# A two-block network on one core: VectorE scales the rows before the transposes, and a new order of the eight feature tiles

## What is computed

```
first network:   h = x
  layer 0        h += even_mixer(rms_norm(h));  h += swiglu(rms_norm(h))
  layer 1        h += odd_mixer(rms_norm(h));   h += moe_swiglu(rms_norm(h))     8 experts, top 2
                 x = rms_norm(h)
second network, twice:
                 x += 0.5 * rms_norm(swiglu(rms_norm(x)))        ("f1")
                 x += rms_norm(hybrid_mix(rms_norm(x)))          (the hybrid mixer)
                 x += 0.5 * rms_norm(swiglu(rms_norm(x)))        ("f2")

rms_norm(x, g) = x * rsqrt(mean(x*x) + 1e-6) * g       row by row
```

## Time and profile before

| | us |
|---|---|
| median of three runs | 2469.18 |
| the profiled execution | 2467.24 |
| its span in the trace | 2465.5 |
| PE busy | 2437.7 (99%) |
| DVE busy | 2034.6 (83%) |
| ACT busy | 1544.8 (63%) |

### The profile page before, as it was taken

The page is one execution under the profiler, slowest core; times in us unless marked ns, Lnnn a source line. Parts: engine busy times, 40 slices in busy tenths (PEclk is TensorE's granted clock), DMA queues, the critical chain, the costliest instruction groups (busy, mean ns, idle before and its releaser), DMA issues.

```text
span 2465.5 us, 39205 instructions
## 1 busy us (share of the span) xinstructions
PE 2437.7 (99%) x14162; PEld 2083.5 (85%) x14162; DVE 2034.6 (83%) x2978; ACT 1544.8 (63%) x2153; POOL 73.2 (3%) x158
## 2 busy tenths in 40 slices
PE   9999999999999999999999999999999999999998
PEld 8888887788888888888888888899888888898887
DVE  7777766889898989998999987789877877798776
ACT  6754555677777777777777764463644644644544
POOL 9000000000000000000000000000000000000000
PEclk9999999999999999999999999999999999999999
DMA  7466643699999999999999966643566566533663
GB/s 213 147 189 187 179 154 128 232 370 367 354 359 375 366 351 359 377 362 352 368 373 365 365 201 195 187 122 103 173 187 195 174 194 187 154 101 115 197 195 111
DMA packets 481949, 596.82 MB, mean 242 GB/s; under 512 B 21922, under 2 KB 313202, under 8 KB 481808
## 3 DMA queue, kind: packets, MB, share of 16 engines
q1 hardware_dynamic: 478208, 589.47, 71.4%
q0 software_dynamic: 3600, 5.48, 0.8%
HBM read 593.83 MB, written 1.05 MB: 241 GB/s over the span
## 4 chain that ended last, share of the span: by engine, by line
PE 91%; DVE 5%; ACT 2%; issue 1%; DMA 0%; SPq 0%; DVEq 0%; ACTq 0%
PE bank L893 25%; PE bank L654 16%; PE bank L919 12%; PE bank L688 10%; PE bank L660 8%; PE bank L639 5%; PE bank L636 2%; PE bank L1524 1%; DVE wlo_ring L2248 1%; PE bank L904 1%; PE bank L1241 1%; PE bank L1069 1%; PE bank L736 1%; PE bank L760 1%; DVE h L2598 1%
## 5 line engine op out<-in xcount | busy, mean ns | idle before, releaser
L2248 DVE TENSOR_TENSOR wlo_ring<-raw_ring,whi_ring 128x1024 fp32r<-128x1024 f32 (+1 forms) x1122 | 1331.3, 1219 | 116.0 <-ACT whi_ring L1616 96.0
L1616 ACT CAST whi_ring<-raw_ring 128x1024 fp32r<-128x1024 f32 (+1 forms) x1122 | 1145.5, 1051 | 165.2 <-DMA raw_ring<-in_od_exp_w_dram 153.3
L654 PE MATMUL bank<-x,whi_ring 128*128 128x512 f32 x1720 | 427.3, 391 | 0.0
L654 PEld LDWEIGHTS bank<-x,whi_ring 128*128 128x128 f32 x1720 | 315.6, 188 | 60.9
L660 PEld LDWEIGHTS bank<-x,wlo_ring 128*128 128x128 f32 x1720 | 220.9, 191 | 9.4 <-DVE wlo_ring L2248 1.0
L660 PE MATMUL bank<-x,wlo_ring 128*128 128x256 f32 x1720 | 223.8, 283 | 0.8 <-DVE wlo_ring L2248 0.8
L1690 ACT COPY arena<-bank 128x256 f32<-128x256 f32 x110 | 40.9, 372 | 268.8 <-PE bank L660 268.8
L639 PE MATMUL bank<-x,whi_ring 128*128 128x256 f32 (+2 forms) x1024 | 193.0, 289 | 0.7 <-DVE x L2326 0.6
L893 PE MATMUL bank<-whi_ring,xg0hi 128*128 128x512 f32 x448 | 178.3, 398 | 2.9 <-DVE xg0lo L2397 2.9
L893 PE MATMUL bank<-whi_ring,xg1hi 128*128 128x512 f32 x448 | 177.2, 395 | 0.0
L893 PE MATMUL bank<-whi_ring,xg0lo 128*128 128x512 f32 x448 | 175.5, 392 | 0.0
(11 more groups left out here) (540 smaller groups left out, 3576.0 us busy)
## 6 DMA issues: line engine op xcount, KB each, us to landing
raw_ring<-in_od_exp_w_dram SPq DMA_DIRECT2D x672, 512.0 KB, 5.5
raw_ring<-in_ffn_w_gate_dram SPq DMA_DIRECT2D x88, 512.0 KB, 3.9
raw_ring<-in_ffn_w_up_dram SPq DMA_DIRECT2D x88, 512.0 KB, 5.0
raw_ring<-in_ffn_w_down_dram SPq DMA_DIRECT2D x88, 512.0 KB, 3.5
raw_ring<-in_ev_ffn_w_dram SPq DMA_DIRECT2D x66, 512.0 KB, 4.0
raw_ring<-in_w_in_dram SPq DMA_DIRECT2D x42, 512.0 KB, 4.1
raw_ring<-in_od_w_in_dram SPq DMA_DIRECT2D x24, 512.0 KB, 4.3
raw_ring<-in_ev_w_in_dram SPq DMA_DIRECT2D x20, 512.0 KB, 7.0
```

The source lines that it names most:

```text
L654: mm_ = mm(bank[:, :], wh[:, kt, :], X2[:, kt, :, :].rearrange("p a n -> p (a n)"), start=(start and kt == 0), stop=(stop and kt == KT - 1 ...
L1616: nc.scalar.copy(WHI[:, slot, 0:n], RAW[:, slot, 0:n]).then_inc(s["hi_ready"], 1)
L2248: V_.tensor_tensor(WLO[:, slot, 0:n], RAW[:, slot, 0:n], WHI[:, slot, 0:n].bitcast(F32), ALU.subtract)\
```

## The change

- `norm` on DVE no longer writes `DIAG`. It writes the scaled rows themselves to `HN`, in two halves of 512 columns (128x512, two factors), each with an increment of the semaphore, which is renamed from `diag_ready` to `rooted`.
- PE turns `HN` by plain transposes (`turn_block`, 16 instructions), and waits for `rooted` before blocks 0 and 2 of each row tile.
- In the hybrid entries the squares of row tile 1 are made in two halves on ACT. DVE adds epsilon to the first half's sum (`y_mean`), ACT takes the root of the second half's sum with that as its bias. The first entry keeps whole tiles (`by_half=False`).
- `X_ORDER` becomes (0, 2, 1, 3, 4, 6, 5, 7), for every entry.

```diff
-X_ORDER = (0, 2, 4, 6, 1, 3, 5, 7)
+X_ORDER = (0, 2, 1, 3, 4, 6, 5, 7)
...
-            def turn_block(banks, t, b):
+            def turn_block(banks, t, b, rows=H):
                 for kt in (2 * b, 2 * b + 1):
                     last = tr(BANK[banks[b]][:, (2 * (kt % 2) + t) * P:(2 * (kt % 2) + t + 1) * P],
-                              H[:, t, kt * P:(kt + 1) * P], IDENT[:, :])
+                              rows[:, t, kt * P:(kt + 1) * P], IDENT[:, :])
...
                 for t in range(TT):
-                    pe.wait_ge(s["diag_ready"], nxt("diag_ready"))
-                    for last in turn_t(t):
+                    for b in range(4):
+                        if b % 2 == 0:
+                            pe.wait_ge(s["rooted"], nxt("rooted"))
+                        last = turn_block(TURNED, t, b, HN)
                         if t == TT - 1:
                             last.then_inc(s["tp_ready"], 1)
...
+            def norm_by_half(l):
+                act.wait_ge(s["h_ready"], nxt("h_ready"))
+                mean_square(0)
+                act.wait_ge(s["half_ready"], 5 + 3 * l)
+                af(HN[:, 1, 0:512], H[:, 1, 0:512], ACT.Square, scale=D ** -0.5, accum_out=STAT[:, 1:2])\
+                    .then_inc(s["y_ssq"], 1)
+                act.wait_ge(s["h_ready"], nxt("h_ready"))
+                af(HN[:, 1, 512:D], H[:, 1, 512:D], ACT.Square, scale=D ** -0.5, accum_out=STAT[:, 24:25])\
+                    .then_inc(s["ssq_ready"], 1)
+                act.wait_ge(s["y_mean"], nxt("y_mean"))
+                act.wait_ge(s["ssq_ready"], nxt("ssq_ready"))
+                af(STAT[:, 35:36], STAT[:, 24:25], ACT.Sqrt, bias=STAT[:, 25:26]).then_inc(s["root_of_ssq"], 1)
...
-            def norm():
+            def norm(by_half=True):
                 for t in range(TT):
-                    dve.wait_ge(s["ssq_ready"], nxt("ssq_ready"))
-                    link(V_.tensor_scalar(STAT[:, 36 + t:37 + t], STAT[:, t:t + 1], EPS, None, ALU.add))
+                    if t and by_half:
+                        dve.wait_ge(s["y_ssq"], nxt("y_ssq"))
+                        V_.tensor_scalar(STAT[:, 25:26], STAT[:, 1:2], EPS, None, ALU.add).then_inc(s["y_mean"], 1)
+                        dve.wait_ge(s["ssq_ready"], nxt("ssq_ready"))
+                        link(V_.tensor_scalar(STAT[:, 37:38], STAT[:, 24:25], STAT[:, 1:2], EPS, ALU.add, ALU.add))
+                    else:
+                        dve.wait_ge(s["ssq_ready"], nxt("ssq_ready"))
+                        link(V_.tensor_scalar(STAT[:, 36 + t:37 + t], STAT[:, t:t + 1], EPS, None, ALU.add))
                     dve.wait_ge(s["root_of_ssq"], nxt("root_of_ssq"))
                     y, c_ = inverse_root(STAT[:, 34 + t:35 + t], 36 + t, 0.5, 1.5)
-                    V_.tensor_scalar(DIAG[:, t, :], IDENT[:, :], y, c_, ALU.mult, ALU.mult).then_inc(s["diag_ready"], 1)
+                    for h in range(2):
+                        hs = slice(h * 512, (h + 1) * 512)
+                        V_.tensor_scalar(HN[:, t, hs], H[:, t, hs], y, c_, ALU.mult, ALU.mult).then_inc(s["rooted"], 1)
```

More of the change, by code:

```diff
@@ L183, in build @@
         names = """hi_ready lo_ready chunk_used bank_free silu_ready hidhi_made
-        hid_ready half_ready gate_lo gate_sum gate_ready up_lo rx_mm rx_made row_root gate_order lrt_ready hid_made h_ready y_ready y_half ssq_ready root_of_ssq y_ssq y_gained y_mean root_of_y diag_ready tp_ready xhi_ready x_ready ident_ready first_tp first_ready consts_ready cols_tp cols_ready
+        hid_ready half_ready gate_lo gate_sum gate_ready up_lo rx_mm rx_made row_root gate_order lrt_ready hid_made h_ready y_ready y_half ssq_ready root_of_ssq y_ssq y_gained y_mean root_of_y rooted tp_ready xhi_ready x_ready ident_ready first_tp first_ready consts_ready cols_tp cols_ready
         loads_done gbc_used dve_order pool_order router_ready msk_ready pos_mm flag_ready
@@ L692, in spread_roots @@
             def spread_roots():
-                pe.wait_ge(s["diag_ready"], nxt("diag_ready", 2))
+                pe.wait_ge(s["rooted"], nxt("rooted", 2))
                 for t in range(TT):
@@ L2223, in _ @@
                 post(f1)
-                norm()
+                norm_by_half(l)
                 gain(f"mix_pre{l}")
@@ L2300, in ffn_roots @@
                         link(V_.scalar_tensor_tensor(ROOT_D[t], y, c_, ROOT[t], ALU.mult, ALU.mult))
-                        V_.tensor_copy(ROOT[t], ROOT_D[t]).then_inc(s["diag_ready"], 1)
+                        V_.tensor_copy(ROOT[t], ROOT_D[t]).then_inc(s["rooted"], 1)
                         V_.tensor_scalar(ROOT_D[t], ROOT_D[t], D ** -0.5, None, ALU.mult)
                     else:
-                        V_.tensor_tensor(ROOT[t], y, c_, ALU.mult).then_inc(s["diag_ready"], 1)
+                        V_.tensor_tensor(ROOT[t], y, c_, ALU.mult).then_inc(s["rooted"], 1)
                         link(V_.tensor_scalar(ROOT_D[t], y, c_, D ** -0.5, ALU.mult, ALU.mult))
@@ L3261, in _ @@
                 dve.wait_ge(x_loaded[t], 16)
-            norm()
+            norm(by_half=False)
             dve.wait_ge(s["first_ready"], 1)
```

## The result

The changed kernel takes 2473.64 us (median of 20 runs) against 2468.43 us of the kernel before (20 runs): ratio 1.0022, 95% interval 1.0016 to 1.0028, which is 5.4 us more, 3.9 to 6.9 (the two medians differ by 5.2). The profiled execution has a span of 2473.1 us. All medians are of runs in the chip's fast state; one run of e9 (2675.51 us at a granted clock of 0.849) was in the slow one and isn't counted.

What follows compares the result with a forecast made beforehand. PE, busy 99% of the span, bounds the long products, but DVE's chain paces the entries. Plain entries 2.82, experts' leave -0.05, hybrid entries 1.22 and first entry 0.82 sum to +4.8 us: 2469.18 to 2474.0, range 2469.0 to 2478.0.

Steps and rivals of the forecast that it cites:

- What bounds the entries: Ahead of `gain` in a hybrid entry: PE late by only 0.46 us, then DVE's chain sets the pace.
- The write of 512 columns: DVE's write of half a row tile's scaled rows in `norm`: 541 ns, two halves holding DVE 0.91 us instead of 0.26.
- D: Rival: DVE's 512-column write runs at one element a cycle, +2.1 us, 2476.1; chance 0.11.
- The order: `gain` with the new tile order: DVE stands 0.23 us twice, +0.47 in each of six plain entries, 2.82 together.
- B: Rival: slack behind the entries makes the gaps of the new order vanish, +1.0 us, 2470.2; chance 0.15.
- The hybrid entry: Two hybrid entries: first copy of `gain` 0.31 us later through DVE's queue, 0.30 more from the order; +1.22 together.
- The first entry: First entry: longer writes and weight splits put the first subtraction at 11.57 against 11.12, plus two order gaps; +0.82 us.
- rival C: TensorE's clock falls to half in transpose-only stretches of rooted entries, one to three times at about 0.8 us: 2475.6; chance 0.22.
- a stretch of few products: On the path to the experts: said to precede the granted clock's fall to 0.50 at 437.30 to 440.70.
- The 0.2% taken as the border: Whole kernel: a measurement tells about 0.2%, 4.9 us, from no change, putting the border between same and slower at 2474.1.

Runs made afterwards that it cites:

- e9: Kernel before with row tile 0 half by diagonal, half by scaled rows, row tile 1 all by scaled rows, order (0, 2, 4, 1, 6, 3, 5, 7): 2467.64 against 2467.82 us.
- e7: Changed kernel with PE doing row tile 0's eight transposes twice in each of the three rooted entries: 2475.05 us, a single execution read for its trace.
- e10: Changed kernel as it is, profiled once more: 2474.39 us, a single execution read for its trace.
- e3: Kernel before with order (0, 1, 2, 3, 4, 5, 6, 7), each odd tile right behind its even neighbour: 2491.98 against 2468.09 us, ratio 1.0098.
- e4: Kernel before with order (0, 2, 4, 1, 6, 3, 5, 7), two other tiles between neighbours: 2467.27 against 2468.09 us, ratio 0.9998.
- e2: Kernel before with only the new order (0, 2, 1, 3, 4, 6, 5, 7): 2474.07 against 2468.09 us, ratio 1.0022.
- e1: Changed kernel with the old order (0, 2, 4, 6, 1, 3, 5, 7) put back: 2469.78 us against 2468.09 for the kernel before, ratio 1.0008.
- e5: Changed kernel with DVE making `y_mean` ahead of row tile 0's writes in the hybrid entries: 2472.86 us, a single execution read for its trace.
- e8: Changed kernel without PE's unread products (`keep_busy`) ahead of the hybrid entries: 2472.88 us, a single execution read for its trace.
- e6: Kernel before, old order, with only row tile 1 by scaled rows and plain transposes, row tile 0 by diagonal: 2467.31 against 2467.15 us, ratio 0.9998.
- e11: Kernel before as it is, profiled once more: 2468.08 us, a single execution read for its trace.

## Why the prediction was right

*What bounds the entries:* right. PE was late by about half a microsecond only, and the saved half of its turning time came back as idle time (0.68 before the first release then, 0.88 and 1.08 now). e7 shows it directly.

*The write of 512 columns:* 541 ns predicted; the median of the twelve is 544, and two in a row take 1.00 us, so they start 0.46 apart. D, with 0.75, falls.

*The order:* 0.47 a plain entry predicted; 0.45 to 0.50 measured in all but the second dense entry (and the router's wider stage in e10). e3 shows the same wait at full size, e4 that a place more removes it. B, the free order, falls by e2.

*The hybrid entry:* 0.61 predicted, 0.65 and 0.66 measured; the rows alone give 0.19 (e1) and the order alone 0.40 (e2), 0.59 together. The step by step working holds too: from DVE's first write to ACT's root 1.09 worked out and 1.10 measured, to the first copy 3.24 and 3.27. That ACT's half squares would wait for the bias behind DVE's writes is plain in the trace (1.14 idle) and e5 takes it away.

*The first entry:* 0.82 predicted, 0.79 and 0.86 measured. The working put the first subtraction 3.96 behind DVE's first write (11.57 less 7.61); e10, which starts at 7.61 as before did, has 3.99. In the first profile it starts at 11.55, but there DVE began at 7.50, so 4.05 behind: the near match of that clock time, and of 0.79, has luck in it.

*Where it was short:* the sum was 4.8 and the traces give 5.2 and 5.4, the timed runs 5.4 with their interval. That the forecast of 2474.0 lies only 0.4 from the measured 2473.64 is partly luck: it started from 2469.18, the median of three runs, where twenty give 2468.43, and this 0.75 made up for the 0.4 to 0.6 that the sum lacked. Two things are outside the sum. First, the second dense entry lost 0.72 instead of 0.47. The extra 0.25 is DVE standing 0.28 us ahead of its update of `H`, behind one of its own small instructions:

```profile
1761.05 1.41 DVE L2621 SCALAR_TENSOR_TENSOR h<-arena,stat,h 128x512 f32<-128x512 f32 x2 [0.28 <-DVE stat L2617]
```

It stands at the same place, 0.28 each time, in e1, e7, e8 and e10, and in none of before, e2 to e6, e9 and e11. e9 has a like stand of 0.34 at another place (ahead of L3019 at 1645.75, behind DVE's own copy). It comes again with the same kernel and no wait of the code explains it; its cause stays open. Second, the clock: rival C was no case by itself but an addition, in three of ten hybrid entries, at 0.3 to 0.8 us each; by these ten an estimate of 0.3 us in the mean of an execution. In the first profile of the changed kernel it didn't fall in a hybrid entry at all, and it never fell in the first entry, which the prediction held to be alike. A fall was priced at 0.8; with the new order, two of two were nearer 0.3, the size that the prediction gave for the case in which DVE sets the pace (about 0.4). And the prediction's reading that the clock fell at 437.30 after "a stretch of few products" is loose: PE was busy 2.67 us of the 3.30 before it.

The forecast gave slower a chance of 0.55, and slower it is: 1.0022, with an interval of 1.0016 to 1.0028 that is clear of no change. The 0.2% taken as the border of what can be told was too wide: the interval of twenty runs on each side reaches 0.06% to either side.

## What to carry to other kernels

When two engines work through the same banks in turn, the second use of a bank is released by the other engine's work on the first. The distance between the two in the order has to be at least the way round (copy, subtraction, releases) over the pace of the slower engine: here 1.02 us over DVE's 0.39, so three places. With two places the remainder is lost each time, 1.02 - 0.78 = 0.24, twice an entry here; with one place 1.02 - 0.39 = 0.63, four times an entry (e3's 2.5). Every stage that shares the order pays it. And before work is moved from a busy engine to another, ask which of them is late at that point, and what small instruction will stand behind the new long one: here a bias of 0.15 us, behind 0.9 us of writes, took back what the squares in halves should have given, and 0.29 us of it came back in e5.

## What the runs showed of the hardware

- TensorE's clock fell from 1.00 to 0.50 of 2.4 GHz in three of ten hybrid entries, each time after a stretch in which PE had only fp32 transposes and was idle for half of it (busy 1.59, 1.72 and 1.47 us of 3.40). The same stretch in e5's other entry (busy 1.72) brought no fall. The Trainium skill (TensorE: Matmul & The Clock Gate, Part 4: PE-mode transpose) says that transposes don't count for the clock as products do. The falls don't contradict it, but with half of each stretch idle they don't show it either; against a strict reading speak e7, where PE had 3.4 us of nothing but transposes (busy 3.10) at 1.00 and no fall behind them, and the leave of the experts, at 1.00 with sixteen transposes in 3.4 us.
- With 5.4 us of idle PE ahead of the transposes (e8) it fell in both entries, before the first transpose.
- What 3.4 us at half the clock cost depends on who sets the pace: 0.3 us in a hybrid entry with the new order. On the way into the experts, where PE sets it (products of 512 columns start 0.43 us apart at the half clock and 0.23 at the full one), the fall lasted 6.8 us instead of 3.4 in e6 and e7, and the splits behind it came 1.4 and 1.3 later.
- The stage whose weights come in fastest (the experts, some 360 GB/s) varied by up to 3.1 us between executions. That is more than half of the 5.4 measured here, and the count of weight splits, stage by stage, told the two apart.
